# Down projections as seven block products, with the hidden rows in spans of 512

## The reference

```
def macaron_ffn(x, g_pre, w_gate, w_up, w_down, g_post):
    n = rms_norm(x, g_pre)
    f = (jax.nn.silu(n @ w_gate) * (n @ w_up)) @ w_down
    return x + 0.5 * rms_norm(f, g_post)
```

## Time and profile before

| what | us |
|---|---|
| median of three runs | 1622.4 |
| span of the profiled execution, first to last instruction | 1623.4 |
| PE busy in it | 1597.7 |
| DVE busy | 1006.0 |
| ACT busy | 702.3 |
| POOL busy | 186.3 |

### The profile page before, as it was taken

How to read it: one execution, slowest core, us unless ns; L and a number is a source line. 1 busy time by engine, 2 the same in 40 slices (tenths; PEclk the granted TensorE clock), 3 DMA queues, 4 the chain that set the end, 5 groups by cost and what they waited for, 6 DMA issues and landing times.

```text
span 1623.4 us, 28759 instructions
## 1 busy us (share of the span) xinstructions
PE 1597.7 (98%) x12010; PEld 1550.8 (96%) x12010; DVE 1006.0 (62%) x1296; ACT 702.3 (43%) x1209; POOL 186.3 (11%) x167
## 2 busy tenths in 40 slices
PE   7999999999999999999999999999999999999998
PEld 6999999999999999998989869899999999999998
DVE  5873675477367566999444532786377457637743
ACT  5551453255145444652453433554145325415542
POOL 2020220121022000000010110011022012102200
PEclk9999999999999999999999999999999999999999
DMA  5132323223232331233343452114223223322321
GB/s 178 53 118 65 94 90 104 79 86 123 61 96 83 125 113 53 79 105 118 105 150 136 178 184 80 53 52 131 76 80 101 82 79 104 105 78 79 104 79 59
DMA packets 137320, 159.04 MB, mean 98 GB/s; under 512 B 3133, under 2 KB 130705, under 8 KB 137192
## 3 DMA queue, kind: packets, MB, share of 16 engines
q1 hardware_dynamic: 131616, 138.16, 27.1%
q0 software_dynamic: 5488, 19.10, 3.4%
q10 hardware_dynamic: 96, 0.02, 0.0%
HBM read 152.22 MB, written 5.40 MB: 97 GB/s over the span
## 4 chain that ended last, share of the span: by engine, by line
PE 90%; DVE 8%; DMA 1%; ACT 1%; issue 0%; SPq 0%; ACTq 0%; DVEq 0%
PE slot L1934 43%; PE slot L2091 39%; DVE f L1721 4%; PE slot L1980 2%; PE slot L1962 1%; PE slot L2326 1%; PE slot L2347 1%; PE slot L1986 1%; PE slot L2383 1%; DMA raw<-in_ffn_w_gate_dram 1%; PE slot L1994 1%; DVE wp L1307 1%; DVE f L1337 1%; DVE f L1728 1%; PE slot L2368 0%; PE slot L2310 0%
## 5 line engine op out<-in xcount | busy, mean ns | idle before, releaser
L2091 PE MATMUL slot<-nb,wu 128*128 128x288 f32 x4704 | 630.9, 295 | 0.0
L2091 PEld LDWEIGHTS slot<-nb,wu 128*128 128x128 f32 x4704 | 628.4, 188 | 0.0
L1934 PE MATMUL slot<-mid,wp 128*128 128x288 f32 x3648 | 497.3, 297 | 3.4 <-DVE wp L1307 1.7
L1934 PEld LDWEIGHTS slot<-mid,wp 128*128 128x128 f32 x3648 | 489.4, 189 | 7.7 <-issue 4.5
L744 ACT ACTIVATE wp<-raw 128x1024 fp32r<-128x1024 f32 x104 | 109.4, 1059 | 304.7 <-PE slot L1934 278.5
L1307 DVE TENSOR_TENSOR wp<-raw,wp 128x1024 fp32r<-128x1024 f32 x104 | 127.0, 1222 | 99.8 <-ACT wp L744 99.7
L667 POOL TENSOR_TENSOR raw<-raw,q 128x512 f32<-128x512 f32 x56 | 81.7, 1459 | 823.9 <-DVE wu L1466 523.1
L1934 PE MATMUL slot<-n,wp 128*128 128x288 f32 x960 | 134.8, 298 | 2.1 <-issue 1.7
L1934 PEld LDWEIGHTS slot<-n,wp 128*128 128x128 f32 x960 | 129.0, 189 | 5.7 <-issue 3.4
L1618 DVE TENSOR_TENSOR f<-slot,f 128x576 f32<-128x576 f32 x48 | 36.3, 757 | 137.5 <-PE slot L1934 137.5
L1476 DVE TENSOR_TENSOR wu<-raw,wu 128x512 fp32r<-128x512 f32 x56 | 38.8, 692 | 91.8 <-ACT wu L882 91.8
(11 more groups left out here) (284 smaller groups left out, 1668.9 us busy)
## 6 DMA issues: line engine op xcount, KB each, us to landing
raw<-in_ffn_w_gate_dram SPq DMA_DIRECT2D x32, 1024.0 KB, 5.3
raw<-in_ffn_w_up_dram SPq DMA_DIRECT2D x32, 1024.0 KB, 5.3
raw<-in_ffn_w_down_dram SPq DMA_DIRECT2D x32, 1024.0 KB, 4.8
raw<-in_mix_w_in_dram SPq DMA_DIRECT2D x8, 1024.0 KB, 5.0
kring<-in_cache_mem_k_dram POOLq DMA_DIRECT2D x6, 1024.0 KB, 5.6
raw<-in_xattn_w_k_dram SPq DMA_DIRECT2D x4, 1024.0 KB, 4.8
raw<-in_xattn_w_v_dram SPq DMA_DIRECT2D x4, 1024.0 KB, 4.8
raw<-in_mix_w_out_dram SPq DMA_DIRECT2D x4, 1024.0 KB, 4.7
```

Of the source, the lines that this page charges most:

```text
L1934: ins = pe.matmul(slot(u)[:, half, 0:HALF], weights(J)[:, wi, kt], X(xi, kt, half), start=kt == 0 and k == 0, stop=kt == KT - 1 and k == l ...
L2091: ins = pe.matmul(dst[:, 0:HALF], wu[:, p, wi, kt], nb[:, p, xi, kt], start=start and kt == 0 and k == 0, stop=kt == KH - 1 and k == len(P ...
```

## The change

The down projections get the seven block products too. The hidden features are now worked on in eight **spans** of 512. A down group multiplies a slab of 512 hidden rows by 512 outputs; its seven products are 12 matmuls each as well, and its results fill whole slots of 2 x 288 columns. Per span there are two down groups and four gate and up groups, in the order gate, down, down, up, gate, up; the down groups belong to the span before. For this the hidden rows are no longer kept as two parts of eight tiles (`mid`) but as the seven operands of the products (`mo`): DVE multiplies gate and up by quarters (C11, C22, C21, C12), makes four sums (`turned`), and ACT and DVE split the quarters and sums.

The outputs are gathered in `f` by quarters, and for all but the first span in pieces: ACT copies P1, P6 and P7 (576 columns each) out of PSUM, POOL adds these copies to `f` or takes them off, and DVE does the same with the four banks that are finished. The squares behind the last group follow the quarters, and so do the gains at the end, which are shared out over ACT, POOL and DVE. The loops on ACT, DVE, POOL and SP are written out. A down slab is loaded by two transfers. The core of the diff: the list of groups, POOL's additions and its order, ACT's, DVE's sums, takes and order (in it, with a minus, the old take of a down tile), and on PE the start of P3 and the last up group, where the first down group's P1 and P5 are cut in two halves, for the span's earlier and later pair of tiles:

```diff
+    found = []
+    for span in range(1, SPANS):
+        places = ((0, 1), (2, 3, 1), (0, 1, 2), (3, 2), (0, 1), (2, 3))
+        if span % 2 == 0:
+            places = [tuple(p ^ 1 for p in of) for of in places]
+        kinds = (("gate", span, 0), ("down", span - 1, 0), ("down", span - 1, 1), ("up", span, 0), ("gate", span, 1), ("up", span, 1))
+        found += [(*kind, of) for kind, of in zip(kinds, places)]
+    return found + [("down", SPANS - 1, 0, (0, 1, 3)), ("down", SPANS - 1, 1, (2, 3, 0))]
...
+                def add_p1(n):
+                    pool.wait_ge(p1_copied, group_count(name, n))
+                    nc.gpsimd.tensor_tensor(f_part(n, 0, 1), f_part(n, 0, 1), part1[:, :, :], ALU.add).then_inc(f11_part, 1)
+                def add_p6(n):
+                    pool.wait_ge(p6_copied, group_count(name, n))
+                    nc.gpsimd.tensor_tensor(f_part(n, 0, 0), f_part(n, 0, 0), part6[:, :, :], ALU.add).then_inc(f12_part, 1)
+                def subtract_p7(n):
+                    pool.wait_ge(p7_copied, group_count(name, n))
+                    pool.wait_ge(c22_done, group_count(name, n))
+                    nc.gpsimd.tensor_tensor(f_part(n, 1, 0), f_part(n, 1, 0), part7[:, :, :], ALU.subtract).then_inc(f22_part, 1)
+                sum_q2(0)
+                sum_q4(0)
+                for n in range(NG):
+                    if n + 1 < NG:
+                        sum_q2(n + 1)
+                    if adds(n):
+                        add_p6(n)
+                    if n + 1 < NG:
+                        sum_q4(n + 1)
+                    if adds(n):
+                        subtract_p7(n)
+                    if adds(n + 1):
+                        add_p1(n + 1)
+                if name == "ffn2":
+                    pool.wait_ge(f_squared, 8 * STAGE[name] + 4)
...
+                def conv_late(n):
+                    pair = pair_of(n)
+                    conv_high("2", pair, (c12_mul, gated_count(name, pair)))
+                    conv_high("4", pair, (s4_sum, pair_count(name, pair)))
...
+                def group(n):
+                    more = n + 1 < NG
+                    copy_p6(n)
+                    if is_kind(n - 1, "gate"):
+                        silu_rest(n - 1)
+                    elif is_kind(n - 1, "up"):
+                        if n - 1 != LAST_UP:
+                            conv_sums(n - 1)
+                            conv_late(n - 1)
+                    if more:
+                        high_q2(n + 1)
+                    copy_p7(n)
+                    if more:
+                        act.wait_ge(p7_done, group_count(name, n))
+                        high_q13(n + 1)
+                        if n != LAST_UP:
+                            copy_p1(n + 1)
+                    if is_kind(n, "up"):
+                        conv_early(n)
+                    if more:
+                        act.wait_ge(p4_done, group_count(name, n))
+                        high_a2(n + 1)
+                    if n == NG - 2:
+                        warm(ACT.Sqrt)
...
+                def conv_low(k, pair):
+                    dve.wait_ge(mo_hi[k], pair_count(name, pair))
+                    V.tensor_tensor(mo_place(k, 1, pair), mo_source(k), mo_place(k, 0, pair).bitcast(F32), ALU.subtract)\
+                        .then_inc(mo_lo[k], 1)
+                def sum_75(pair):
+                    V.tensor_tensor(turned[:, 0:2], quarters(sil)[:, 0:4:3], quarters(sil)[:, 2:3].to_broadcast([P, 2, HALF]),
+                                    ALU.subtract).then_inc(s75_sum, 1)
+                def sum_6(pair):
+                    dve.wait_ge(s75_sum, pair_count(name, pair))
+                    V.scalar_tensor_tensor(out=turned[:, 2], in0=turned[:, 1], scalar=-1.0, in1=quarters(sil)[:, 0],
+                                           op0=ALU.mult, op1=ALU.subtract).then_inc(s6_sum, 1)
+                def sum_4(pair):
+                    dve.wait_ge(s6_sum, pair_count(name, pair))
+                    V.scalar_tensor_tensor(out=turned[:, 3], in0=turned[:, 2], scalar=-1.0, in1=quarters(sil)[:, 1],
+                                           op0=ALU.mult, op1=ALU.subtract).then_inc(s4_sum, 1)
...
+                def late_sum(n):
+                    pair = pair_of(n)
+                    multiply_c12(n)
+                    dve.wait_ge(c12_mul, gated_count(name, pair))
+                    sum_4(pair)
+                def bank(n, role):
+                    return slot(group_use(name, n, role))[:, :, 0:HALF]
+                def take_y(n):
+                    u = group_use(name, n, "y")
+                    if adds(n):
+                        dve.wait_ge(f11_part, down_count(name, n))
+                    else:
+                        dve.wait_ge(p1_copied, group_count(name, n))
+                    dve.wait_ge(p2_done, group_count(name, n))
+                    free(V.tensor_tensor(f_part(n, 0, 1), bank(n, "y"), f_part(n, 0, 1), ALU.add), u)
+                def take_p5(n):
+                    if not adds(n):
+                        dve.wait_ge(p7_copied, group_count(name, n))
+                    elif GROUPS[n][1] > 1:
+                        dve.wait_ge(f22_part, down_count(name, n - 6) if n < NG - 2 else down_count(name, n - 5))
+                    dve.wait_ge(p5_done, group_count(name, n))
+                    V.tensor_tensor(f_part(n, 1, 0), f_part(n, 1, 0), bank(n, "z"), ALU.subtract).then_inc(c22_done, 1)
...
+                def group(n):
+                    more, down, up = n + 1 < NG, is_kind(n, "down"), is_kind(n, "up")
+                    turn = is_kind(n - 1, "up") and n - 1 != LAST_UP
+                    if n and more:
+                        sum_q13(n + 1)
+                    if turn:
+                        late_sum(n - 1)
+                    if adds(n):
+                        take_p5(n)
+                    if down:
+                        take_y(n)
                     else:
-                        dve.wait_ge(mid_ready, MID0[name] + KT + b * KT)
-                        free(V.tensor_tensor(halves(f[:, i]), slot(u)[:, :, 0:HALF], halves(f[:, i]), ALU.add), u)
-                def down(b):
-                    for i in range(KT - 2):
-                        take_down(i, b)
-                        if i:
-                            prepare(J0 + 16 + i + 2, b)
-                    start_groups(GROUPS, b, lambda: take_down(KT - 2, b), lambda: take_down(KT - 1, b))
+                        take_c11(n)
+                    if turn:
+                        conv_low("756", pair_of(n - 1))
+                    if more:
+                        low_q2(n + 1)
+                    if turn:
+                        conv_low("2", pair_of(n - 1))
+                        conv_low("4", pair_of(n - 1))
+                    if down and not adds(n):
+                        take_p5(n)
+                    elif not down:
+                        take_c22(n)
+                    if up:
+                        multiply_c11(n)
+                        multiply_c22(n)
+                    if more:
+                        low_q13(n + 1)
+                    if up:
+                        conv_low("3", pair_of(n))
+                        conv_low("1", pair_of(n))
+                    if more and n != LAST_UP:
+                        low_a2(n + 1)
+                    if up:
+                        multiply_c21(n)
+                        early_sums(n)
+                    if n == LAST_UP:
+                        conv_low("756", pair_of(n))
+                        low_a2(n + 1)
+                    elif n + 2 < NG:
+                        low_a11(n + 2)
+                    if down:
+                        take_x(n)
+                        take_z(n)
+                    else:
+                        take_c12(n)
...
+                def p3(n):
+                    pe.wait_ge(c22_done, count(n))
+                    wait_hidden(n, "3")
+                    pe.wait_ge(q4_lo, count(n))
+                    product(n, P3, z_of(n), False, [job_done, job_done])
...
+                    wait_place(d, "z")
+                    pe.wait_ge(mo_lo["756"], before)
+                    pe.wait_ge(q13_lo, count(d))
+                    product(d, P5, z_of(d), True, [], (0,))
+                    wait_hidden(d, "1")
+                    product(d, P1, x_of(d), False, [p1_done], (1,))
+                    wait_hidden(d, "756")
+                    product(d, P5, z_of(d), False, [p5_done], (1,))
+                    p6(d)
+                    p2(d)
+                    p7(d)
```

1043 lines of the change are left out of this document (562 added, 481 removed).

## The result

| | before | after |
|---|---|---|
| median of the runs, us | 1622.4 | 1688.8 (1686.6 to 1691.4) |
| span of the profiled execution, us | 1623.4 | 1684.7 |
| matmuls | 12010 | 11628 |
| busy of DVE / POOL, us | 1006.0 / 186.3 | 1321.5 / 425.3 |
| feed-forward stages, us | 564.0 and 564.7 | 595.5 and 597.3 |

The change made the kernel slower: 1.0407 times the time before, 95% interval 1.0393 to 1.0422, or +66.5 us where +30.7 was forecast and 1688 was the end of the range. The sign and the mechanism in the repeated spans were right, and the size there came out right because two errors cancel; the edges of the two stages were wrong.

A forecast was written before the change was run, and what follows sets the result against it. PE was taken to bound the kernel, busy 1597.7 of 1623.4 us. Terms -51.2 + 39.0 + 5.0 + 33.6 + 4.3 = +30.7 us gave 1653 against the median of 1622.4; range 1604 to 1688.

The forecast's parts named there:

- What is removed: Down products in both feed-forward stages take 84 matmuls instead of 96: 384 fewer on PE's path, -51.2 us.
- POOL and DVE exclude each other: DVE's two-SBUF-input instructions and POOL's form one queue: 1.11 us per POOL sum, 1.25 per addition of 576 columns.
- that rival: POOL holds the ports for its whole reported time, 0.19 and 0.21 us more each: +46 us, 1699; chance 0.09.
- The ledger of 66.7 in 67.2: Per 512-row span, DVE and POOL work counts 66.7 of PE's 67.2 us, so they cannot hide unless every wait does.
- The group behind an up group: P3 waits 1.5 us for the C22 take, 26 times: +39.0; P5 another 0.4 before down groups, 12 times: +5.0.
- The two down groups: DVE and POOL overrun each span's down groups, delaying PE through P7's copy: 2.8 us a span, 12 times, +33.6.
- The end of each stage: The last pair's splits come late, 2 x 2.1 us, +4.3; the squares behind stay as short as today.
- At the very end: ACT's last four quarters of gains lie beside PE's row sums: nothing, or 1 us if that cover is too short.
- Late, but not adding up: Waits absorb the down groups' lateness, and the C22 take is 0.5 us late: 1619.5 or 1593.5; chance 0.20.
- Full pace: Rival that PE keeps its pace, so the saved products count in full: 1571 us; chance 0.06.

The follow-up runs named there:

- six edits: Changed kernel with both stage edges reordered, late splits, early sum, end squares summed on TensorE, and two VectorE takes moved forward: 1621.2 us.
- seven edits: The six edits, plus TensorE's reordered products for each stage's last pair, with that place's early sum put behind the hidden rows: 1613.2 us.
- P7's copy ahead: Changed kernel with ScalarE's copy of P7 moved ahead of the up group's last two hidden-row splits and the split of Q2: 1754.0 us.
- the take ahead: Changed kernel with VectorE's take of C22 moved ahead of the split of Q2 and the up group's last two hidden-row splits: 1698.7 us.

## Why the prediction was right about the sign and wrong about the size

- **What is removed.** 384 matmuls are gone (12010 to 11628, with two new small ones in the row sums), 25.6 us a stage. Right; loads and straight code cost nothing that the trace shows.
- **POOL and DVE exclude each other.** Right, and nearly in size. At 320.70 the split L1656 takes 2.41 us behind POOL's addition of 320.57, 1.20 over its 1.21, where I had estimated 1.25. DVE is back at 321.90, 0.11 us before the addition's reported end. So the Trainium skill (SBUF — State Buffer, "SBUF: two separate sides"), by whose rule the whole of the addition would be held, is again too long, by 0.11 us here and by 0.13 in the row that I had. The 0.19 and 0.21 a piece at which I priced that rival were too much, since in both rows DVE is ready only after POOL's instruction has started. Its time, 1699, lies nearer to the result than the forecast does, but not for its reason: the spans lost what I had forecast with the shorter hold.
- **The ledger of 66.7 in 67.2.** The conclusion was half right. DVE no longer hid behind PE, but six and seven edits do the same work on DVE and POOL in 68.53 us a span. That the list was full did not decide; what stood in front of what did.
- **The group behind an up group**, +39.0 and +5.0 (12 x 0.4 is 4.8). The place was right, the size too small: of the 26 groups 24 lie in the 12 repeated spans (36.0 + 5.0 forecast), and there 5.1 us a span make 61. P3 is due 8.0 us into the group. With the lateness of P4 in front of it, which waits for the copy of P7, it starts 1.8 us late in the first of the span's two groups (307.65) and 2.6 in the other (357.02), where I had 1.5. The way from the sum of weights to the take was right, 7.20 us in both for my 7.15. What was wrong is where it begins: 2.55 and 3.36 us into the group, not 2.2; in the second of them because DVE's list comes out of the down groups late.
- **The two down groups**, +33.6. Too large: 1.4 us a span, 17 in all. I had let all of their lateness reach PE through the copy of P7. Instead it stays on DVE's list for a while: the sum of weights starts 3.07 us into the up group behind them (337.43, P6 at 334.36), and PE waits only in the gate group after that. So a part of this term is in the one above. That the two errors cancel is luck: 74.6 forecast for the 12 spans, 77.6 measured.
- **The end of each stage**, +4.3 for both (2 x 2.1 is 4.2). This is the step that failed, with the starts of the stages, to which I gave no price of their own. Measured: the ends 22.2 more than before. Of that the last pair is 8.1 (2.05 and 1.81 us, each with 0.1 for the restart, twice), right in kind and half in size. 3.7 are waits for P7's copy in the last two groups. The remaining 10 or so lie behind the last product, where I had written that "the squares behind stay as short as today". They did not: before, one tile of rows was finished at a time; now the last two products complete one half each of two tiles, and their takes stand on DVE's list between the additions of squares and behind the memory rows. The starts lose 14.2 (the 13th group behind an up group, 2.3 a stage, is in that; I had 1.5): the split of A2 stands behind the second pair's sums, 2.4 us late, which I did not look at since the diff seemed only to unroll that part. On the profiled span this makes some 11 for the starts, 18 for the ends and 3 for the repeated spans, about the 31 between +30.7 and +61.3. At the very end the forecast had nothing or 1 us: behind the row sums the kernel takes 15.8 us where it took 14.7. The granted clock is 0.50 there from 1664.5 to 1674.7, behind PE's wait of 4.4 us, where in before it was so from 1609.0 to 1612.4; what that costs is not separated.
- **The rivals.** "Late, but not adding up" is not what the changed kernel does, though half of the 33.6 that it put at nothing did not show in its place; and it is close to what the same work does in another order: six edits stand at 1621. Full pace (1571) none of the kernels reached.

What stays open: each of the wait times at the edges is read from the trace, but only 6.7 and 2.8 us of them were recovered in the changed kernel itself, the second hardly clear of the spread, and seven edits still lose 2.8 us at the last pair and 4.7 behind the last product of the first stage.

## What to carry to other kernels

When work moves onto an engine that runs one list in order, price the stage's first and last groups with their own timelines; cover that a loop's middle has is missing there. Before counting amounts, ask of each step in the list whether it waits and who needs the steps behind it: the same additions cost 32 us in one order and 8 in another. And a late step should not be pulled in front of others if it waits itself; rather push back those that nobody is waiting for. When a reordering makes PE's waits longer, look at the granted clock before blaming the order: with P7's copy ahead 43 of the 65 us were steps at 0.50.

## What the runs showed of the hardware

POOL's hold falls on whatever DVE instruction with two SBUF inputs stands next: it made a split of 288 columns 1.54 us instead of 0.45 and one of 1024 columns 2.41 instead of 1.21. I had not expected that two POOL instructions in a row let DVE in between. POOL's and DVE's timeline in the second down group:

```profile
330.23 1.29 POOL L742 TENSOR_TENSOR raw<-raw 128x512 f32<-128x512 f32 x1 [0.62 <-DVE wu L1651]
331.48 2.42 POOL L755 TENSOR_TENSOR f<-f,part 128x576 f32<-128x576 f32 x1
```

```profile
330.40 2.20 DVE L1646 TENSOR_TENSOR wu<-q,wu 128x1024 fp32r<-128x1024 f32 x1 [0.25 <-ACT wu L985]
332.52 2.46 DVE L1656 TENSOR_TENSOR wu<-raw,wu 128x1024 fp32r<-128x1024 f32 x1
```

L755 follows L742 at once and yet takes 2.42 us where it takes 1.43 at best: the split that waited behind L742 goes first, and the next split waits behind L755. Where both engines have work, as here, they take turns, and each pays for the other's.

PE's granted clock fell to 0.50 behind waits of 1.9 us (10 of 11 times, with the take ahead) and 2.4 us (most of 30 times, with P7's copy ahead), and a step of 133 ns became one of 240. It did not fall behind the wait of 2.2 us at the start of each stage of the changed kernel.
